# The residual's own spread root copied to SBUF by ScalarE ahead of the first FFN

## The reference, cut to what matters

```python
x = first_block(...)                       # ends with rmsnorm(x, final_g)
h = modulate(rms_norm(x, ffn1_norm[l]), sh1, sc1)
x = x + 0.5 * g1[:, None, :] * swiglu(h, ffn1_w_gate[l], ffn1_w_up[l], ffn1_w_down[l])
# swiglu: (silu(h @ w_gate) * (h @ w_up)) @ w_down, 2816 hidden columns
```

## Time and profile before

| | |
|---|---|
| median of 3 runs | 1014.89 us (1014.87 to 1016.33) |
| the profiled execution, its own time | 1017.17 us |
| its span, first to last instruction | 1015.4 us |
| TensorE busy | 975.3 us, 96% |
| VectorE busy | 720.1 us, 71% |
| ScalarE busy | 514.1 us, 51% |
| mean granted TensorE clock | 0.993 |

### The profile page before, as it was taken

The page is one execution under the profiler, slowest core; times in us unless marked ns, Lnnn a source line. Parts: engine busy times, 40 slices in busy tenths (PEclk is TensorE's granted clock), DMA queues, the critical chain, the costliest instruction groups (busy, mean ns, idle before and its releaser), DMA issues.

```text
span 1015.4 us, 19280 instructions
## 1 busy us (share of the span) xinstructions
PE 975.3 (96%) x8063; PEld 956.4 (94%) x8063; DVE 720.1 (71%) x1007; ACT 514.1 (51%) x756; POOL 42.4 (4%) x68
## 2 busy tenths in 40 slices
PE   6999999989999999999899999998997999999997
PEld 5999999989998999999899999998997999999997
DVE  4778877667848755676999888787966666465555
ACT  4654365456553455644754474566274454444442
POOL 2100000000000013311000000000000000000000
PEclk9999999999999999999999999999997999999999
DMA  9987586735866786487367786774323356474721
GB/s 366 365 273 257 201 295 251 279 106 173 295 217 225 244 298 208 147 308 232 139 234 277 248 306 223 276 267 148 125 96 113 126 166 228 147 255 152 251 90 42
DMA packets 138990, 219.55 MB, mean 216 GB/s; under 512 B 7177, under 2 KB 110970, under 8 KB 138904
## 3 DMA queue, kind: packets, MB, share of 16 engines
q1 hardware_dynamic: 136576, 213.94, 61.3%
q10 hardware_dynamic: 1336, 2.64, 0.7%
q0 software_dynamic: 992, 1.76, 0.7%
HBM read 217.25 MB, written 1.05 MB: 215 GB/s over the span
## 4 chain that ended last, share of the span: by engine, by line
PE 81%; DVE 8%; ACT 3%; DMA 3%; issue 3%; ACTq 0%; SPq 0%; DVEq 0%
PE pw L564 56%; PE pacc L564 25%; DVE ACC L1610 2%; DVE WL L1594 2%; ACT AR L1135 1%; DMA ring<-in_ada_w 1%; DMA ring<-in_odd_in_w 1%; ACT WH L1135 1%; DVE SQT L1690 1%; DVE hl L1695 1%; DMA cst<-in_consts 1%; DMA ring<-in_odd_out_w 1%; DVE AR L1610 0%; ACT hh L1135 0%; ACT SQT L1135 0%
## 5 line engine op out<-in xcount | busy, mean ns | idle before, releaser
L1135 ACT ACTIVATE WH<-ring 128x1024 fp32r<-128x1024 f32 x288 | 301.6, 1055 | 281.0 <-PE pw L564 146.3
L1594 DVE TENSOR_TENSOR WL<-ring,WH 128x1024 fp32r<-128x1024 f32 x288 | 347.2, 1223 | 90.3 <-ACT WH L1135 89.7
L564 PE MATMUL pw<-hh,WH 128*128 128x256 f32 x1408 | 372.8, 286 | 8.6 <-DVE WL L1594 2.8
L564 PE MATMUL pw<-hh,WL 128*128 128x256 f32 x1408 | 368.8, 283 | 0.0
L564 PE MATMUL pw<-hl,WH 128*128 128x256 f32 x1408 | 285.3, 284 | 0.0
L564 PEld LDWEIGHTS pw<-hh,WH 128*128 128x128 f32 x1408 | 270.5, 192 | 14.6 <-issue 10.5
L564 PEld LDWEIGHTS pw<-hh,WL 128*128 128x128 f32 x1408 | 270.8, 192 | 0.0
L564 PEld LDWEIGHTS pw<-hl,WH 128*128 128x128 f32 x1408 | 219.8, 192 | 0.3
L564 PE MATMUL pacc<-YH,WH 128*128 128x256 f32 x672 | 192.7, 287 | 3.4 <-issue 2.5
L564 PE MATMUL pacc<-YL,WH 128*128 128x256 f32 x672 | 190.7, 284 | 0.0
L564 PE MATMUL pacc<-YH,WL 128*128 128x256 f32 x672 | 190.6, 284 | 0.0
(11 more groups left out here) (264 smaller groups left out, 798.5 us busy)
## 6 DMA issues: line engine op xcount, KB each, us to landing
ring<-in_w_mod SPq DMA_DIRECT2D x72, 512.0 KB, 4.6
ring<-in_odd_in_w SPq DMA_DIRECT2D x56, 512.0 KB, 6.1
ring<-in_ada_w SPq DMA_DIRECT2D x48, 512.0 KB, 6.7
ring<-in_ffn_w_gate SPq DMA_DIRECT2D x44, 512.0 KB, 4.5
ring<-in_ffn_w_up SPq DMA_DIRECT2D x44, 512.0 KB, 4.9
ring<-in_ffn_w_down SPq DMA_DIRECT2D x44, 512.0 KB, 4.8
ring<-in_even_in_w SPq DMA_DIRECT2D x40, 512.0 KB, 7.4
ring<-in_even_out_w SPq DMA_DIRECT2D x16, 512.0 KB, 5.6
```

Of the source, the lines that this page charges most:

```text
L564: return eng.matmul(o, a, b, start=start, stop=stop, skip_group_check=True)
L1135: return eng.activation(dst, src, func, **kw)
L1594: tt(WL[:, i % NL, :], slot(half_of(i)), WH[:, i % NH, :].bitcast(F32), SUB).then_inc(s_lo, 1)
```

## The change

Behind the first four of ScalarE's eight `hh` of the seam stands a copy of the 128x256 spread root `xnew` from PSUM to SBUF, at `XNW`, a stretch of the arena that the gate product of the FFN's fourth block uses later; the eight products of `update_x` read it there. The bank of `xnew` counts as free when ScalarE has copied it. `xnew_back` idles three steps in place of four, and ScalarE's silu of block 3, which writes over `XNW`, waits for the end of `update_x`.

```diff
+        XNW = ar(512 * 3, T)
@@ TensorE
             def xnew_back():
-                yield from idle(4)
+                yield from idle(3)
                 back("xnew")
...
-            spread("xnew", 8, 4, (s_x, 24), True)
+            spread("xnew", 8, 4, None, True)
@@ ScalarE
                         if blk >= 4:
                             s.wait_ge(s_yl, y0 + blk - 3)
+                        elif blk == 3 and tag == "f1":
+                            s.wait_ge(s_x, X_FIN[L_F1])
...
-            modulate(L_F1, M2[:, 0:8])
+            modulate(L_F1, M2[:, 0:8], range(4))
+            evac("xnew", XNW, src=pw[place["xnew"]][:, 0:T])
+            modulate(L_F1, M2[:, 0:8], range(4, 8))
@@ VectorE
             def update_x():
-                v.wait_ge(*full["xnew"])
+                v.wait_ge(*gone["xnew"])
                 v.wait_ge(s_hl, 8 * L_F1 + 8)
                 for k in range(8):
-                    stt(out=xT[:, k, :], in0=xT[:, k, :], scalar=fg[:, k:k + 1], in1=pw[place["xnew"]][:, 0:T],
+                    stt(out=xT[:, k, :], in0=xT[:, k, :], scalar=fg[:, k:k + 1], in1=XNW,
                         op0=MUL, op1=MUL).then_inc(s_x, 1)
```

## The result

The changed kernel is slower: ratio 1.0042, interval 1.0030 to 1.0054. Its median of 5 runs is 1020.85 us (1019.38 to 1021.20), beside 1016.30 us (1014.87 to 1017.88) for the kernel before. Forecast were 2.5 us more and 1017.4 us, range 1015.4 to 1019.3. The direction was right, the size too small: 4.3 us by the ratio, and the time lies beyond the range. Of the 3.5 us between 1017.4 and 1020.85, 1.4 are the kernel before itself, whose median was 1014.89 us when the forecast was worked out and 1016.30 here; the other 2.0 are the change. The profiled execution took 1020.85 us, its span 1018.9 us, 3.5 above that of before; the mean granted clock was 0.990.

The account below looks back on a forecast made before the run. TensorE, busy 96% of the span, was taken as the bound. 1.55 us gained, 1.35 lost, 0.24 gained and 2.92 lost made 2.5 us later, 1017.4 us on the median; range 1015.4 to 1019.3.

Parts of the forecast that it names:

- The stall that goes: TensorE's 2.76 us wait for a bank at block 1, about 495 us, goes; copy 0.05 us, update_x unchanged.
- What VectorE lets through: VectorE's low parts, 512 to 527 us, let TensorE keep 1.55 of 2.76 us; 1.21 lost to waits for WL.
- bt03: Transpose between the halves of f1g5 and f1u5 waits for ScalarE's copy of bt01: a stall of 1.35 us.
- the first rival: Landing for f1d4 does not move with VectorE, bt03 waits 1.55 us longer: +4.0, 1018.9 us; 7%.
- bt11: Transpose behind ada11 in f1d4's first half waits for ScalarE's copy of bt10, 3.49 us after f1u5: stall 2.92 us.
- the model: Block 4, with VectorE idle, gave the path from the up product's end to bt11: 3.45 us plus 0.04.
- Neither clash: Rival: neither bt03 nor bt11 waits, the gain VectorE lets through stays: 1.79 us faster, 1013.1; 10%.
- only the first: Rival: bt03 waits but bt11's bank is free: 0.44 us faster, 1014.5; 6%.
- the landing does not move: Rival: landing for f1d4 does not come sooner with VectorE, bt03 waits 1.55 us longer: +4.0, 1018.9; 7%.
- VectorE is faster with SBUF operands: Rival: VectorE is faster or catches up, lead and landing move up to 2.76 us: +1.3 to +2.0, about 1016.5; 7%.
- The full lead of 2.76 us: Rival: VectorE is no limit and no clash occurs, 2.76 + 0.24 = 3.0 us faster, 1011.9; 4%.

Follow-up runs that it names:

- e6: Changed kernel with transposes kept in their old places and update_x's eight products on 16 of 256 columns, residual then wrong; ratio 0.9951 to the kernel before.
- e5: Changed kernel plus 12 spare matmuls of 128 columns ahead of ada11's sum, while bt11 waits; ratio 1.0013 to the kernel before.
- e2: Kernel before with only the side queue idling 5 steps for 6, so transposes come one half-piece earlier; xnew stays in PSUM; ratio 1.0068 to the kernel before.
- e11: Changed kernel unaltered, one more single profiled execution to look at its granted clock; 1021.20 us, no comparison of times.
- e12: Changed kernel unaltered, a second single profiled execution to look at its granted clock; 1024.38 us, no comparison of times.
- e4: Changed kernel with the list of banks turned by one before bt11, which takes f1b50's bank in place of bt10's; ratio 0.9983 to the kernel before.
- e3: Changed kernel plus 26 spare matmuls of 128 columns ahead of ada11's sum, while bt11 waits; ratio 1.0045 to the kernel before.
- e8: Changed kernel with ScalarE's copies of the bt banks also one half-piece earlier, idle 11 for 12; ratio 0.9976 to the kernel before.
- e9: Kernel before unaltered, one more single profiled execution to look at its granted clock; 1020.78 us, no comparison of times.
- e7: Changed kernel with transposes in their old places and VectorE's S5 weights two side steps later, two later idle steps dropped; ratio 0.9960 to the kernel before.
- e1: Changed kernel with the side queue behind xnew_back idling 7 steps for 6, so transposes keep their old places; ratio 0.9977 to the kernel before.

## Why the prediction was right in direction and too small

**The stall that goes.** Right: no hole at 495 us. ScalarE's copy took 0.36 us and moved no matmul of TensorE. `update_x` with SBUF operands took 478 ns a product, from PSUM 474 in the kernel before: no gain, as the earlier trace rows said. The Trainium skill, "VectorE: DVE Perf Modes", section on the TRN2 errata, gives fewer fixed cycles to SBUF; for this form neither kernel shows it.

**What VectorE lets through.** Right in mechanism (e6 shows it by relieving VectorE), 0.25 us off in size: the lead from 560 us on is 1.30, not 1.55. 1.62 of 2.92 us were lost in place of 1.21 of 2.76. Of these the view of waits names 0.3 us at 514.5 and 0.4 at 523.9 as waits for WL; the rest goes in smaller pieces that it does not name, but e6 gives them back as well.

**bt03.** Right: behind the copy of bt01, itself behind the landing for `f1d4` and a WH. The landing did move with VectorE, so the first rival is out. The hole was 1.14 us in place of 1.35. Counted on the clock of the kernel before, bt03 started at 573.82 + 1.90 = 575.72 where 575.54 was forecast: 0.18 later. That it came out so near is partly luck. In the other profiles with this wait the hole was 1.12 us (e5), 1.35 (e2), 1.52 and 1.53 (e11, e12), 1.68 (e4) and 1.77 (e3): it follows the load of `f1d4`, which takes 4.48 us in the chain of the change and 5.11 in that of e3.

**bt11.** The place and the cause were right, and e4 and e8 each remove this wait alone or with the other. The path was taken 0.4 us too short: from the end of `f1u5` at 580.67 (577.78 + 2.89) to bt11 at 584.56 it was 3.89 us, not 3.49, and the hole 3.34 us, not 2.92. Most of the difference is ScalarE's YH. In the block that I took as the model it started 0.09 us behind VectorE's second product (564.43); here (timeline of ScalarE) it started at 582.36, and the product pair of 581.24 had taken 0.75.
```profile
580.75 0.66 ACT L1137 ACTIVATE AR<-pw 128x256 f32<-128x256 f32 x2 [1.82 <-PE pw L566]
582.36 0.63 ACT L1137 ACTIVATE YH<-AR 128x512 fp32r<-128x512 f32 x1 [0.95 <-DVE AR L2130]
582.90 1.04 ACT L1137 ACTIVATE WH<-ring 128x1024 fp32r<-128x1024 f32 x1
583.84 0.58 ACT L1137 ACTIVATE AR<-pw 128x512 f32<-128x512 f32 x1
```
From the end of the product pair, 581.99, to YH that is 0.37 us, 0.28 more than in the model. Every profile of a kernel with the new copy has 0.37 to 0.38 at this place and 0.1 at its other blocks, save e8, in which ScalarE's steps are moved; the kernel before (three profiles) and e2 have 0.1 here too. As e2 has the same two waits and its bt11 waited 3.1 us in place of 3.3, the delay doesn't come from the waits. What causes it stays open.

**The step that failed** is the last sentence of the rivals: a fall of the clock "has a price too, but after the present 2.76 us stall the granted clock stays at full speed". From one execution I concluded that such a stall is free, and let a new one of nearly 3 us cost its length alone. It cost its length and 1.50 us of half clock behind it (e5; the falls of e2, e9 and e11 cost 1.49 to 1.50 too). The stretch of TensorE adds up: 2.5 forecast, 0.18 for bt03, 0.42 for bt11 and 1.49 for the clock make 4.6, and 4.61 was measured. This holds for the one execution: the other two of the changed kernel stand at +4.96 and +5.95 (e11, e12), by bt03's longer wait and, in e12, the longer fall.

**What lies beyond.** Between the steady stretch and the end the change lost another 0.8 us. Of it 0.51 are another fall of the clock at about 694 us, where TensorE works in short pieces; it is in all three profiles of the changed kernel and in e2, e5 and e7, and in none of the three of the kernel before nor in e1, e3, e4, e6 and e8. The other 0.3 us lie in the mixer. There the clock falls in every profile between 760 and 790 us, and how long it stays at half differs: 10.2 us in all in the three profiles of the kernel before, in the changed one, e2 and e3; 6.8 us in e1, e4, e5, e6, e8 and e11; 3.4 us in e7 and e12. From 705 us to the end the first group is within 0.3 us of the kernel before, the second gains 1.2 to 1.7 us on it, the third 2.4 to 2.5. Executions of the same changed kernel are found in all three groups, so a gain or loss of 1 to 2.5 us between two profiles can come from here alone. What decides which execution gets which of these falls is not settled. The kernel before also pays 1.5 us in some executions for its own stall, which the profile shown ahead of the prediction did not; that may be why kernels without this stall do better in their times than their steady shifts say, but it is not shown how much of it this is.

**The rivals.** "Neither clash" and "only the first" are out by the chain. So are "the landing does not move", by the chain of bt03, and "VectorE is faster with SBUF operands", by its 478 ns. The full lead of 2.76 us exists only where VectorE is relieved (e6).

## What to carry to other kernels

When a held buffer is given back earlier by taking a step out of a shared queue, everything behind it in that queue moves as well: pad the queue to keep the old places (e1), or move the queue that empties the buffers too (e8). Price a new wait of about 3 us on TensorE with what its clock may do behind it, and take more than one execution before calling a stall of this length free. Where the lead is limited by another engine, moving that engine's side work out of the stretch keeps more of it: 2.06 us in place of 1.00 here (e7, e1).

## What the runs showed of the hardware

A wait of 3.1 to 3.3 us in an otherwise solid stream of matmuls was followed by half clock for 3.4 to 6.8 us in all four profiles that have it (the change, e2, e11, e12). In three of them the clock was full through the whole wait and fell 0.8 to 0.9 us behind it; in e12 it fell 2.0 us into the wait. A stall of 2.8 us was followed by a fall in one of three executions of the same kernel. 2.84 us of unneeded matmuls ahead of the wait (which left a hole of 0.68 us) kept the clock at full. The Trainium skill, "Perfetto Trace Analysis", section Matmul Optimizations, says that the engine scales its power by how much it is used, and that matmuls should therefore "execute back-to-back in batches". e5 agrees, and puts the price of one such fall here at 1.50 us.
